# Attention masks added by TensorE as a matrix product instead of by VectorE, and the sink's exponential in one instruction

## The chip, the cores and the metric

The kernel runs on one core of one Trainium2 chip, as one program. The metric is the device time of one execution in microseconds (us). Before the change it was 1840.17 us, the median of 3 runs (1836.04 to 1841.17).

A core has engines with an instruction queue each, which run side by side and meet through semaphores: TensorE (PE: matrix products into the accumulation memory PSUM; PEld is its loading of the stationary operand), VectorE (DVE), ScalarE (ACT), GpSimd (POOL), and SyncE (SP), which here only starts transfers.

## The reference

Two transformer blocks of depth 2 over 256 tokens of width 1024, in fp32. The first block has a gated linear attention layer and a latent attention layer (MLA), the second two grouped-query attention layers (GQA). Every layer also attends to 256 memory tokens. Two kinds of attention are masked: MLA is causal, and the first GQA layer attends within a band of 128 positions and has a sink per head.

```python
# first block, layer 1 (MLA): 8 heads, key width 128 + 64 (rope), queries in blocks of 128
#   softmax over the keys with kpos <= qpos
# second block, layer 0: 12 heads of width 64, 3 key heads
def banded_attention(q, k, v, radius, sink=None):
    ...
    mask = abs(qpos - kpos) <= radius
    s = einsum(q, k) * ATTN_SCALE
    s = where(mask, s, -inf)
    m = maximum(max(s), sink)
    p = exp(s - m)
    denom = sum(p) + exp(sink - m)
    o = einsum(p, v) / denom
# second block, layer 1: the same heads, no mask and no sink
# memory attention: 4 heads in each layer, no mask and no sink
```

## The kernel before

The 256 tokens are two tiles (t = 0, 1) of 128 rows. All weights stream through in 534 units of 128 x 1024 numbers: SP loads a unit into `raw` (3 slots), ACT rounds it to `whi`, DVE forms the remainder `wlo` (6 slots each), and PE multiplies in three fp32r passes (`act_hi`*`whi`, `act_hi`*`wlo`, `act_lo`*`whi`). Work is written out by hand once per engine: each engine has a class `Stages` with a method per stage, and `model` calls them in the same order. The order on an engine is the order of that code, and the counts in the semaphore waits tie the engines together.

`attention(jobs)` is such a method on PE, ACT and DVE. A job is one head. There are four calls: 4 memory heads (gated linear layer), 4 memory heads and 8 causal heads (MLA), 4 memory heads and 12 banded heads (first GQA layer), and the same without mask (second GQA layer). The heads go through a pipeline of steps s = 0, 1, ...; the buffers `prob`, `top`, `inv`, `es` and the score banks `ps[:, j % 4]` hold 4 heads.

- **PE, step s** (lines 1886 to 1940): score products of head s, both query tiles (L1901; in MLA a second product for the 64 rope rows, L1904); transposes of the probabilities of head s-3 (L1925), which wait for `prob_ready`; product with the values of head s-4 (L1937), which waits for `probT_ready`. Where heads are 64 wide (both GQA layers), the scores of two heads are issued together at every even s, alternating between them: one head's operands lie in partitions 0 to 63, the other's in 64 to 127. A new score group waits until the exponentials of the head that used its bank are done. A plain fp32 product is two MATMUL instructions here.
- **DVE, step s** (lines 1450 to 1516): waits for the scores of head s (`score_done`). For a masked head it adds the mask to them and writes the sum into `prob` (L1465 causal, one instruction per tile; L1468 band, one instruction). Then the maximum (L1473, L1476), the negated and scaled maximum `top` (L1481, or L1488 and L1490 with a sink); after that the normalising of head s-2 (L1499 with a sink, L1501, L1504) and the low part of the output of head s-5 (L1513).
- **ACT, step s** (lines 905 to 953): waits for `top` of head s-1, then two exponentials (L924, each followed by a short instruction that reads its sum), with a sink one more small exponential before each of them (L921, into `es`); then the copy of the transposes of head s-4 from PSUM (L937, L941) and the high part of the output of head s-5 (L951).

For a masked head the exponential reads `prob` (SBUF), for another one the scores in PSUM. After the last heads PE goes on with the first output projection units (L1609), which are in the ring already.

Of the kernel before, what the change touches and what calls it, by code (L numbers as in the profile page):

```python
# [21 lines left out]
P = 128  # L22
# [242 lines left out]
def build(nc, units, x_in, mem_in, mem2_in, const_in, gain_in, row_in, alpha_in, post_in, out):  # L265
    NU = units.shape[0]
    with ExitStack() as ctx:
# [40 lines left out]
        alpha = sb("alpha", [GRANK, 512])  # L308
        lowT = sb("lowT", [GRANK, S])
# [72 lines left out]

        gla_pe = sem("gla_pe")
# [56 lines left out]
        def mla_jobs():  # L440
            jobs = []
            for h in range(MH):
# [4 lines left out]
                                 causal=True, mask=constant("causal"), sink=None, rms=("qn", h)))  # L447
            return jobs

        def gqa_jobs(b):  # L450
# [7 lines left out]
            for h in range(QH):  # L458
# [4 lines left out]
                                 mask=constant("band") if b == 0 else None,  # L463
# [148 lines left out]
        def _(act):  # L612
            class Stages:
# [197 lines left out]
                def gla(self):  # L811
                    act.wait_ge(params_landed, 48)
                    self.split(7)

# [94 lines left out]
                def attention(self, jobs, beside={}):  # L909
                    n, base = len(jobs), self.jobs  # L910
                    for s in range(n + 5):
                        if 1 <= s <= n:

                            j, job = s - 1, jobs[s - 1]
                            act.wait_ge(top_ready, base + j + 1)
                            for t in range(TT):
                                n_keys = keys_of(job, t)
                                src = (ps[:, j % NB, t * S:t * S + n_keys] if job["mask"] is None
                                       else prob[:, j % NB, t, 0:n_keys])
                                if job["sink"] is not None:  # L920
                                    nc.scalar.activation(es[:, j % NB, t:t + 1], job["sink"], ACT.Exp,  # L921
                                                         bias=top[:, j % NB, t:t + 1])
# [35 lines left out]
        def _(dve):  # L958
            V = nc.vector

            class Stages:
# [488 lines left out]
                def attention(self, jobs, beside={}):  # L1450
                    n, base = len(jobs), self.jobs
                    for s in range(n + 5):
                        if s < n:
# [4 lines left out]
                            if job["mask"] is not None:  # L1458
                                if j >= NB:
                                    dve.wait_ge(probT_done, base + j - NB + 1)  # L1460
                                mask = job["mask"].rearrange("p (t k) -> p t k", t=TT)
                                for t in range(TT):
                                    n_keys = keys_of(job, t)
                                    if job["causal"]:
                                        ins = V.tensor_tensor(prob[:, j % NB, t, 0:n_keys], src[:, t, 0:n_keys],  # L1465
                                                              mask[:, t, 0:n_keys], ALU.add)
                                if not job["causal"]:
                                    ins = V.tensor_tensor(prob[:, j % NB], src, mask, ALU.add)  # L1468
                                self.step(ins)
                                src = prob[:, j % NB]  # L1470
# [507 lines left out]
```

## Time and profile before

| | before |
|---|---|
| median of 3 runs | 1840.17 us (1836.04 to 1841.17) |
| profiled execution, first to last instruction (span) | 1837.2 us, mean granted clock 0.980 |
| PE busy | 1718.0 us (94%), 10778 matmul instructions |
| DVE busy | 1095.9 us (60%) |
| ACT busy | 899.6 us (49%) |
| POOL busy | 76.6 us (4%) |
| DMA | 289.20 MB, 157 GB/s over the span |
| chain that ended last, by engine | PE 81%, DVE 9%, ACT 5% |

In the rows of stretches below, each row has the stretch from start to end, its length, the busy time (and instructions) of PE, PEld, DVE, ACT and POOL, the granted share of TensorE's clock (PEclk: 1.00 is 2.4 GHz, 0.50 is 1.2 GHz), the busy share of the DMA engines and GB/s. In rows of a timeline stand the start, the time until the last of the x instructions ended, and in brackets how long the engine had stood idle and who ended it. The profile gives the profiled execution's span and no other time of it; the median stands 3.0 us above that span. The PE row counts a matmul as busy until its result is written, so a busy PE isn't one at its peak. The weights' products (L1609, L1675 to L1677, L1706) make up most of PE's time; the masked attention heads lie in two stretches, about 912 to 940 us (MLA) and 1244 to 1288 us (first GQA layer).

### The profile page before, as it was taken

How to read it: one execution, taken by the hardware profiler on the slowest of the kernel's cores; microseconds unless marked ns; L12 is line 12 of the kernel's file. 1: busy time of each engine (PE TensorE's matmuls, PEld its weight loads, DVE VectorE, ACT ScalarE, POOL GpSimd, SP SyncE). 2: the span in 40 equal slices, each digit the busy share in tenths (PEclk: the TensorE clock that was granted, in tenths of full speed). 3: DMA queues.
4: the chain of work that ended last, by engine and by line, in shares of the span. 5: the costliest groups of instructions: out<-in, count | busy, mean ns of one | idle time of the engine just before them, and what ended most of it. 6: DMA issues, size and time to landing. Idle time of an engine off the chain costs nothing.

```text
span 1837.2 us, 29340 instructions
## 1 busy us (share of the span) xinstructions
PE 1718.0 (94%) x10778; PEld 1516.3 (83%) x10778; DVE 1095.9 (60%) x1613; ACT 899.6 (49%) x1430; POOL 76.6 (4%) x99
## 2 busy tenths in 40 slices
PE   7999999889999999999799999996899998889998
PEld 6999887579999899987678999873699986579997
DVE  4555666455555655567765555558565556755554
ACT  5444453445444544445555444456544444754443
POOL 1000000000000100001201000000100000110000
PEclk9999999999999999999899999999999998999999
DMA  6655444245555455545224555550255553145553
GB/s 210 194 192 183 162 148 138 92 160 161 188 183 187 149 184 185 182 158 184 80 96 155 190 184 186 170 174 1 97 201 193 179 184 107 47 138 190 185 185 114
DMA packets 79654, 289.20 MB, mean 157 GB/s; under 512 B 8928, under 2 KB 9184, under 8 KB 79216
## 3 DMA queue, kind: packets, MB, share of 16 engines
q1 hardware_dynamic: 78272, 282.23, 46.4%
q0 software_dynamic: 1008, 5.24, 0.8%
q10 hardware_dynamic: 320, 1.01, 0.2%
q8 instruction: 34, 0.56, 0.1%
q14 instruction: 20, 0.16, 0.0%
HBM read 287.39 MB, written 1.05 MB: 157 GB/s over the span
## 4 chain that ended last, share of the span: by engine, by line
PE 81%; DVE 9%; ACT 5%; issue 2%; DMA 2%; POOL 1%; SPq 0%; DVEq 0%; ACTq 0%
PE ps L1706 18%; PE ps L1609 16%; PE ps L1677 13%; PE ps L1675 13%; PE ps L1676 13%; DVE wlo L981 2%; PE ps L1555 2%; PE ps L1937 2%; PE ps L1901 1%; DMA raw<-units 1%; ACT whi L637 1%; DVE inv L1476 1%; DVE act_lo L992 1%; ACT junk L660 1%; ACT act_hi L648 1%
## 5 line engine op out<-in xcount | busy, mean ns | idle before, releaser
L1675 PE MATMUL ps<-act_hi,whi 128*128 128x256 f32 x2112 | 603.1, 286 | 4.0 <-DVE wlo L981 3.1
L1676 PE MATMUL ps<-act_lo,whi 128*128 128x256 f32 x2112 | 599.8, 284 | 0.0
L1677 PE MATMUL ps<-act_hi,wlo 128*128 128x256 f32 x2112 | 599.7, 284 | 0.0
L1157 DVE TENSOR_TENSOR wlo<-raw,whi 128x1024 fp32r<-128x1024 f32 x358 | 437.0, 1221 | 177.9 <-ACT whi L777 177.7
L1675 PEld LDWEIGHTS ps<-act_hi,whi 128*128 128x128 f32 x2112 | 407.4, 193 | 10.9 <-DVE wlo L981 3.7
L777 ACT ACTIVATE whi<-raw 128x1024 fp32r<-128x1024 f32 x358 | 365.7, 1052 | 101.9 <-DMA raw<-units 100.9
L1676 PEld LDWEIGHTS ps<-act_lo,whi 128*128 128x128 f32 x2112 | 407.4, 193 | 4.7
L1677 PEld LDWEIGHTS ps<-act_hi,wlo 128*128 128x128 f32 x2112 | 407.2, 193 | 0.0
L981 DVE TENSOR_TENSOR wlo<-raw,whi 128x1024 fp32r<-128x1024 f32 x176 | 211.9, 1226 | 116.0 <-ACT whi L637 115.5
L1126 DVE TENSOR_TENSOR prob<-ps,prob 128x512 f32<-128x512 f32 x132 | 91.3, 692 | 252.8 <-PE ps L1677 252.6
L637 ACT ACTIVATE whi<-raw 128x1024 fp32r<-128x1024 f32 x176 | 180.9, 1055 | 119.2 <-DMA raw<-units 114.1
L756 ACT ACTIVATE sil<-prob 128x256 f32<-128x256 f32 x132 | 55.4, 420 | 343.5 <-DVE prob L1126 343.5
L1609 PE MATMUL ps<-whi,act_hi 128*128 128x512 f32 (+2 forms) x514 | 175.9, 403 | 18.4 <-DVE x L1206 6.3
L1609 PE MATMUL ps<-wlo,act_hi 128*128 128x512 f32 (+2 forms) x514 | 170.7, 393 | 0.0
L1609 PE MATMUL ps<-whi,act_lo 128*128 128x512 f32 (+2 forms) x514 | 170.1, 392 | 0.0
L1706 PE MATMUL ps<-whi,hid_hi 128*128 128x512 f32 x528 | 165.5, 395 | 2.1 <-DVE hid_lo L1132 2.1
L1706 PE MATMUL ps<-wlo,hid_hi 128*128 128x512 f32 x528 | 163.6, 391 | 0.0
L1706 PE MATMUL ps<-whi,hid_lo 128*128 128x512 f32 x528 | 163.1, 390 | 0.0
L1609 PEld LDWEIGHTS ps<-whi,act_hi 128*128 128x128 f32 x514 | 97.0, 194 | 44.9 <-issue 20.5
L759 ACT ACTIVATE hid_hi<-hid 128x256 fp32r<-128x256 f32 x132 | 55.1, 418 | 134.3 <-DVE hid L1120 134.3
L1706 PEld LDWEIGHTS ps<-wlo,hid_hi 128*128 128x128 f32 x528 | 99.1, 188 | 22.1
L1706 PEld LDWEIGHTS ps<-whi,hid_lo 128*128 128x128 f32 x528 | 99.1, 188 | 21.6
(187 smaller groups left out, 1522.2 us busy)
## 6 DMA issues: line engine op xcount, KB each, us to landing
raw<-units SPq DMA_DIRECT2D x534, 512.0 KB, 3.4
arena<-mem_in POOLq DMA_DIRECT2D x3, 1024.0 KB, 6.8
gpost<-post_in POOLq DMA_DIRECT2D x4, 512.0 KB, 4.8
x<-x_in SPq DMA_DIRECT2D x2, 512.0 KB, 4.6
out<-x SPq DMA_DIRECT2D x2, 512.0 KB, 3.2
const<-const_in ACTq DMA_DIRECT2D x1, 816.0 KB, 4.5
row<-row_in ACTq DMA_DIRECT2D x1, 134.0 KB, 5.1
const<-const_in SPq DMA_DIRECT2D x1, 64.0 KB, 3.0
```

The lines of the kernel that those rows point to most:

```text
L637: nc.scalar.activation(whi[:, u % RING, :], raw[:, u % RAW, :], ACT.Copy).then_inc(hi_ready, 1)
L756: nc.scalar.activation(sil[:, c % 2, :], gate_up_rms[:, c % 2, 0, :], ACT.Silu).then_inc(sil_ready, 1)
L759: nc.scalar.activation(hid_hi[:, c % 2, :], hid[:, c % 2, :], ACT.Copy).then_inc(hid_hi_ready, 1)
L777: nc.scalar.activation(whi[:, u % RING, :], raw[:, u % RAW, :], ACT.Copy).then_inc(hi_ready, 1)
L981: V.tensor_tensor(wlo[:, u % RING, :], raw[:, u % RAW, :], whi[:, u % RING, :].bitcast(F32), ALU.subtract).then_inc(lo_ready, 1)
L1126: V.tensor_tensor(gate_up_rms[:, c % 2], ps[:, 4 + c % 2, :].rearrange("p (e s) -> p e s", e=2), inv_rms.unsqueeze(1).to_broadcast([P, 2, ...
L1157: V.tensor_tensor(wlo[:, u % RING, :], raw[:, u % RAW, :], whi[:, u % RING, :].bitcast(F32), ALU.subtract).then_inc(lo_ready, 1)
L1609: ins = T.matmul(ps[:, bank, 0:b - a], a_part[:, t * P:(t + 1) * P], w_part[:, self.slot, w0 + a:w0 + b], start=k == 0 and s0, stop=k == n ...
L1675: T.matmul(out_, whi[:, slot, w], act_hi[:, k, :], start=k == 0, stop=False)
L1676: T.matmul(out_, whi[:, slot, w], act_lo[:, k, :], start=False, stop=False)
L1677: ins = T.matmul(out_, wlo[:, slot, w], act_hi[:, k, :], start=False, stop=k == KD - 1)
L1706: ins = T.matmul(ps[:, 2 * t + j, :], h_part[:, c % 2, tok], w_part[:, slot, j * 512:(j + 1) * 512], start=first and s0, stop=last and s1)
```

## The change

1. In the gated linear layer ACT makes four 128 x 128 fp32r arrays once, behind its first 7 weight units and ahead of an exponential over 1024 columns: the identity `eye`, the two pieces of the band mask that are not zero, and the triangular piece of the causal mask (both tiles use the same).
2. On PE each score group of a masked head gets one more product: `eye` (stationary) times the mask piece (moving, 128 columns), accumulated onto the 128 of the 256 score columns where the mask isn't zero. It's issued once per head and query tile, right behind that tile's score product: 2 for each of 8 heads in MLA, 2 for each of 12 heads in the first GQA layer. It spans all 128 partitions.
3. DVE doesn't add masks any more (L1465, L1468 go), and takes the maximum from PSUM. With the addition goes its wait on `probT_done`.
4. ACT takes the exponentials of masked heads from PSUM. The sink's exponential is one instruction over both tiles' columns instead of two.
5. PE waits once for the four arrays (`masks_ready`) ahead of a masked attention stage.

```diff
@@ -306,6 +306,9 @@
         gain = sb("gain", [P, GAIN_W])
         row = sb("row", [P, ROW_W])
         alpha = sb("alpha", [GRANK, 512])
+        eye = sb("eye", [P, P], F32R)
+        mask_band = sb("mask_band", [P, TT, P], F32R)
+        mask_causal = sb("mask_causal", [P, P], F32R)
         lowT = sb("lowT", [GRANK, S])
         decay = sb("decay", [P, 4 * GH])
         sums = sb("sums", [P, STAT_W])
@@ -380,6 +383,7 @@
         head_hi = sem("head_hi")
         head_lo = sem("head_lo")
 
+        masks_ready = sem("masks_ready")
         gla_pe = sem("gla_pe")
         gla_act = sem("gla_act")
 
@@ -444,7 +448,8 @@
                 jobs.append(dict(q=[m_k[:, t, h * P:(h + 1) * P] for t in range(TT)], k=m_kT[:, h, :],
                                  more=([m_qrT[r, h // 2, t * P:(t + 1) * P] for t in range(TT)], m_krT[r, :]),
                                  v=[m_v[:, t, h * MDV:(h + 1) * MDV] for t in range(TT)], rows=(0, MDV), kt=h,
-                                 causal=True, mask=constant("causal"), sink=None, rms=("qn", h)))
+                                 causal=True, mask=[(t * S + t * P, mask_causal[:]) for t in range(TT)],
+                                 sink=None, rms=("qn", h)))
             return jobs
 
         def gqa_jobs(b):
@@ -460,7 +465,8 @@
                 jobs.append(dict(q=[b_qT[r, h // 2, t * P:(t + 1) * P] for t in range(TT)], k=b_kT[r, g, :],
                                  more=None, v=[b_p[:, t, QKW + g * HD:QKW + (g + 1) * HD] for t in range(TT)],
                                  rows=(r.start, HD), kt=h // 2, causal=False,
-                                 mask=constant("band") if b == 0 else None,
+                                 mask=[(t * S + (1 - t) * P, mask_band[:, t, :]) for t in range(TT)]
+                                 if b == 0 else None,
                                  sink=row[:, ROW_AT["sink"] + h:ROW_AT["sink"] + h + 1] if b == 0 else None,
                                  rms=("bq", h) if b == 1 else None))
             return jobs
@@ -610,6 +616,13 @@
 
         @block.scalar
         def _(act):
+            def round_masks():
+                nc.scalar.activation(eye[:], ident, ACT.Copy)
+                band = constant("band")
+                for t in range(TT):
+                    nc.scalar.activation(mask_band[:, t, :], band[:, t * S + (1 - t) * P:t * S + (2 - t) * P], ACT.Copy)
+                nc.scalar.activation(mask_causal[:], constant("causal")[:, 0:P], ACT.Copy).then_inc(masks_ready, 1)
+
             class Stages:
                 u = used = 0
                 g = th = 0
@@ -811,6 +824,7 @@
                 def gla(self):
                     act.wait_ge(params_landed, 48)
                     self.split(7)
+                    round_masks()
 
                     act.wait_ge(gla_dve, 2)
                     self.step(nc.scalar.activation(at_arena(G_B, 1024), at_arena(G_B, 1024), ACT.Exp))
@@ -913,13 +927,11 @@
 
                             j, job = s - 1, jobs[s - 1]
                             act.wait_ge(top_ready, base + j + 1)
+                            if job["sink"] is not None:
+                                nc.scalar.activation(es[:, j % NB, :], top[:, j % NB, :], ACT.Exp, bias=job["sink"])
                             for t in range(TT):
                                 n_keys = keys_of(job, t)
-                                src = (ps[:, j % NB, t * S:t * S + n_keys] if job["mask"] is None
-                                       else prob[:, j % NB, t, 0:n_keys])
-                                if job["sink"] is not None:
-                                    nc.scalar.activation(es[:, j % NB, t:t + 1], job["sink"], ACT.Exp,
-                                                         bias=top[:, j % NB, t:t + 1])
+                                src = ps[:, j % NB, t * S:t * S + n_keys]
                                 scale = HD ** -0.5 if job["rms"] is None else query_scale(job)[:, t:t + 1]
                                 ins = nc.scalar.activation(prob[:, j % NB, t, 0:n_keys], src, ACT.Exp, scale=scale,
                                                            bias=top[:, j % NB, t:t + 1],
@@ -1455,19 +1467,6 @@
                             j, job = s, jobs[s]
                             dve.wait_ge(score_done, base + j + 1)
                             src = ps[:, j % NB, :].rearrange("p (t k) -> p t k", t=TT)
-                            if job["mask"] is not None:
-                                if j >= NB:
-                                    dve.wait_ge(probT_done, base + j - NB + 1)
-                                mask = job["mask"].rearrange("p (t k) -> p t k", t=TT)
-                                for t in range(TT):
-                                    n_keys = keys_of(job, t)
-                                    if job["causal"]:
-                                        ins = V.tensor_tensor(prob[:, j % NB, t, 0:n_keys], src[:, t, 0:n_keys],
-                                                              mask[:, t, 0:n_keys], ALU.add)
-                                if not job["causal"]:
-                                    ins = V.tensor_tensor(prob[:, j % NB], src, mask, ALU.add)
-                                self.step(ins)
-                                src = prob[:, j % NB]
                             if job["causal"]:
                                 for t in range(TT):
                                     ins = V.tensor_reduce(inv[:, j % NB, t:t + 1], src[:, t, 0:keys_of(job, t)],
@@ -1883,6 +1882,8 @@
 
                 def attention(self, jobs, beside={}):
                     n, base = len(jobs), self.jobs
+                    if any(job["mask"] is not None for job in jobs):
+                        pe.wait_ge(masks_ready, 1)
                     self.done = {job["kt"]: base + j + 1 for j, job in enumerate(jobs)}
                     self.banks_free()
                     self.all_taken()
@@ -1899,10 +1900,13 @@
                                     job, n_keys = jobs[j], keys_of(jobs[j], t)
                                     scores = ps[:, j % NB, t * S:t * S + n_keys]
                                     ins = T.matmul(scores, job["q"][t], job["k"][:, 0:n_keys], start=True,
-                                                   stop=job["more"] is None)
+                                                   stop=job["more"] is None and job["mask"] is None)
                                     if job["more"] is not None:
                                         ins = T.matmul(scores, job["more"][0][t], job["more"][1][:, 0:n_keys],
-                                                       start=False, stop=True)
+                                                       start=False, stop=job["mask"] is None)
+                                    if job["mask"] is not None:
+                                        at, mask = job["mask"][t]
+                                        ins = T.matmul(ps[:, j % NB, at:at + P], eye[:], mask, start=False, stop=True)
                                     if t == TT - 1:
                                         ins.then_inc(score_done, 1)
                         if s in beside:
```

PE in the first GQA layer, one pair of banded heads with what follows it, before (`arena` holds queries, keys and values; the first number of a shape is the rows of the result):

```order
L1901 MATMUL ps<-arena 128x256 x4
L1925 MATMUL ps<-const,prob 128x128 x4
L1937 MATMUL ps<-probT,arena 64x256 x2
L1925 MATMUL ps<-const,prob 128x128 x4
L1937 MATMUL ps<-probT,arena 64x256 x2
```

And the same place now:

```order
L1902 MATMUL ps<-arena 128x256
L1909 MATMUL ps<-mask_band,eye 128x128
L1902 MATMUL ps<-arena 128x256
L1909 MATMUL ps<-mask_band,eye 128x128
L1902 MATMUL ps<-arena 128x256
L1909 MATMUL ps<-mask_band,eye 128x128
L1902 MATMUL ps<-arena 128x256
L1909 MATMUL ps<-mask_band,eye 128x128
L1929 MATMUL ps<-const,prob 128x128 x4
L1941 MATMUL ps<-probT,arena 64x256 x2
L1929 MATMUL ps<-const,prob 128x128 x4
L1941 MATMUL ps<-probT,arena 64x256 x2
```

Four score products of two heads stood next to each other; now a mask product over all partitions stands behind each of them.

PE in MLA, one causal head, before:

```order
L1901 MATMUL ps<-arena 128x128
L1904 MATMUL ps<-arena 128x128
L1901 MATMUL ps<-arena 128x256
L1904 MATMUL ps<-arena 128x256
L1925 MATMUL ps<-const,prob 128x128 x3
```

And now:

```order
L1902 MATMUL ps<-arena 128x128
L1905 MATMUL ps<-arena 128x128
L1909 MATMUL ps<-mask_causal,eye 128x128
L1902 MATMUL ps<-arena 128x256
L1905 MATMUL ps<-arena 128x256
L1909 MATMUL ps<-mask_causal,eye 128x128
L1929 MATMUL ps<-const,prob 128x128 x3
```

The mask product comes in behind the 64-row rope product of each tile, ahead of the next product over all partitions.

## Rows read from the trace of the kernel before

**Rows 1.** Stretches of the first GQA layer: us, busy by engine, PEclk, DMA.

```profile
1244.35:1251.38 7.03, 5.43 (x25) 3.04 (x25) 5.06 (x16) 3.96 (x15) 0.00 (x0) 0.84 0.00 0
1251.38:1258.30 6.92, 5.09 (x26) 2.65 (x25) 5.85 (x19) 4.71 (x17) 0.00 (x0) 0.89 0.01 2
1258.30:1265.46 7.16, 5.33 (x25) 2.95 (x24) 5.35 (x16) 4.08 (x15) 0.00 (x0) 0.86 0.00 1
1265.46:1271.77 6.31, 4.47 (x25) 2.46 (x24) 5.90 (x19) 4.64 (x16) 0.00 (x0) 1.00 0.00 0
...
1278.08:1287.52 9.44, 6.19 (x33) 3.34 (x32) 8.60 (x30) 7.56 (x25) 0.00 (x0) 1.00 0.00 1
```

**Rows 2.** Busy time of a stretch: the eight causal heads' steps, MLA.

```profile
912.09:936.92 24.83, 24.83 (x122) 17.03 (x121) 17.56 (x69) 15.16 (x53) 0.00 (x0) 1.00 0.00 1
```

**Rows 3.** Timeline of DVE, first GQA layer: start, us, engine, line, operation.

```profile
1266.73 0.67 DVE L1468 TENSOR_TENSOR prob<-ps,const 128x512 f32<-128x512 f32 x1
1267.44 0.69 DVE L1476 TENSOR_REDUCE inv<-prob 128x2 f32<-128x512 f32 x1
...
1268.42 0.17 DVE L1490 TENSOR_SCALAR top<-inv 128x2 f32<-128x2 f32 x1
...
1269.99 0.69 DVE L1468 TENSOR_TENSOR prob<-ps,const 128x512 f32<-128x512 f32 x1
```

**Rows 4.** Timeline of ACT in the same cycle.

```profile
1268.63 0.29 ACT L921 ACTIVATE es<-row,top 128x1 f32<-128x1 f32 x1 [0.68 <-DVE top L1490]
...
1269.32 0.28 ACT L921 ACTIVATE es<-row,top 128x1 f32<-128x1 f32 x1
1269.51 0.49 ACT L924 ACTIVATE prob<-prob,top 128x256 f32<-128x256 f32 x1
...
1270.12 0.60 ACT L941 ACTIVATE probT<-ps 128x512 f32<-128x512 f32 x1
```

**Rows 5.** Timeline of PE in the same cycle (rows*columns of the array, then the operand).

```profile
1265.46 1.14 PE L1901 MATMUL ps<-arena 64*128 64x256 f32 x8
1266.54 0.66 PE L1925 MATMUL ps<-const,prob 128*128 128x128 f32 x4
...
1270.77 1.08 PE L1937 MATMUL ps<-probT,arena 128*64 128x256 f32 x4 [0.55 <-ACT probT L941]
1271.77 1.13 PE L1901 MATMUL ps<-arena 64*128 64x256 f32 x8
```

**Rows 6.** Timeline of PE in one causal head's step, MLA.

```profile
929.23 0.70 PE L1901 MATMUL ps<-arena 128*128 128x256 f32 x2
929.86 0.70 PE L1904 MATMUL ps<-arena 64*128 64x256 f32 x2
930.49 0.55 PE L1925 MATMUL ps<-const,prob 128*128 128x128 f32 x3
930.87 0.82 PE L1937 MATMUL ps<-probT,arena 128*128 128x256 f32 x4
931.53 0.28 PE L1901 MATMUL ps<-arena 128*128 128x128 f32 x1
```

**Rows 7.** Timeline of PE, fp32r products of 512 and 192 columns in turn.

```profile
834.28 0.50 PE L1609 MATMUL ps<-wlo,act_hi 128*128 128x512 f32 x2
834.62 0.50 PE L1609 MATMUL ps<-whi,act_lo 128*128 128x512 f32 x2
```

**Rows 8.** Timeline behind MLA's last causal scores, PE and DVE.

```profile
936.65 0.62 DVE L1465 TENSOR_TENSOR prob<-ps,const 128x128 f32<-128x128 f32 x2 [0.57 <-PE ps L1904]
...
937.30 0.61 DVE L1473 TENSOR_REDUCE inv<-prob 128x1 f32<-128x128 f32 x2
...
938.83 0.55 PE L1925 MATMUL ps<-const,prob 128*128 128x128 f32 x3 [1.08 <-DVE prob L1504]
```

**Rows 9.** Timeline of ACT where the change puts its four copies.

```profile
255.96 1.06 ACT L816 ACTIVATE arena<-arena 128x1024 f32<-128x1024 f32 x1 [2.33 <-DVE arena L1232]
```

**Rows 10.** Groups by line, operation and shape: ACT's 128x128 copies.

```profile
L937 ACT ACTIVATE probT<-ps 128x128 f32<-128x128 f32 x8 | 2.1, 266 | 0.0
```

## The prediction

> **What bounds the kernel now.** I read the shares by engine first: PE is busy for 94% of the span, DVE 60%, ACT 49%. So DVE work that goes is worth something only where PE waits for DVE, and PE work that comes costs wherever PE doesn't wait. That has to be read from the two masked stretches, not from the sums.
>
> MLA: over its causal heads PE is busy for the whole 24.83 us [rows 2], DVE for 17.56 of them. PE sets the pace there, a head's step takes 24.83 / 8 = 3.1 us, and DVE waits for PE, as its 0.57 us of idling before the addition shows [rows 8]. Only behind the last scores does PE wait for DVE (1.08 us at L1925 [rows 8]).
>
> First GQA layer: from one masked score group to the next it is 7.03, 6.92, 7.16, 6.31 and 6.31 us (the fifth reads like the fourth), then 9.44 us until the output projection starts [rows 1]. The first three have a PEclk of 0.84 to 0.89, so 2.2, 1.5 and 2.0 us of them ran at 1.2 GHz (twice the missing share times the length). At the full clock the pace is 6.31 us a pair, and it is DVE's: 5.90 us busy, two head steps of it in a row, the second starting 3.26 us behind the first (1266.73 to 1269.99 [rows 3]). PE is busy for 4.47 us of the 6.31 and waits.
>
> **MLA, part by part.** Removed: DVE's additions, about 0.65 us a head (936.65 to 937.30 [rows 8]). They lie beside PE, so for seven of eight heads they are worth 0.
> Added on PE: two mask products a head. First what a product costs when the occupied rows of the array change. Two MATMULs of 256 columns in the value product plus two of 128 take 0.66 us from start to start (930.87, 931.53 [rows 6]), that is 0.22 for 256 columns and 0.11 for 128. But the same pair of 256 columns takes 0.63 when it stands between a 128-row and a 64-row product (929.23, 929.86, 930.49 [rows 6]) instead of 0.44. So each change between 64 and 128 rows costs 0.2 us: about 0.09 until the array is empty and about 0.11 for a load of 128 columns that can't be hidden any more. The mask product comes behind the 64-row rope product, where a change to 128 rows stood anyway. The number of changes stays at four a head; what is added is the mask product's own slot. For a row of 128 columns whose load overlaps, the nearest rows are the transposes: three in 0.38 us with 0.06 of first load, 0.11 each [rows 6]. That is the load's time, and I take it: 2 x 0.11 = 0.22 a head.
> Bounds: the streaming alone. The fp32r passes over 512 and 192 columns follow each other in 0.34 us [rows 7], so 704 columns run near one per cycle of 2.4 GHz (0.29 us), and a narrow one isn't stretched; 128 columns are 0.05 us below. Above: as long as an fp32 MATMUL of 256 columns, 0.22 us.
> Seven heads: 7 x 0.22 = 1.5 us. At the last head the result comes later by the first mask (0.11) and by its own (0.11 of load and a drain that now ends later, 0.26 together), DVE is earlier by 0.65: PE's wait shrinks by 0.3. MLA: 1.5 - 0.3 = +1.2 us.
>
> **First GQA layer, part by part.** Removed from DVE: 0.71 us a head (1266.73 to 1267.44 [rows 3]). Removed from ACT: the second sink exponential, 0.19 us (1269.32 to 1269.51 [rows 4]), and 0.03 for reading PSUM instead of SBUF (an estimate; both kinds of exponential lie near 0.49).
> Added on PE: today the eight MATMULs of two heads take 1.08 us with the entry (1265.46 to 1266.54 [rows 5]), which is 8 x 0.11 + 0.2: the two heads run side by side in the halves of the array, since one alone needs 0.22 a piece. A mask product over 128 rows now stands behind each score product. So no two heads' products are neighbours, and every product stands behind a change of rows. Four score products at 0.63 = 2.5; four mask products at 0.09 + 0.11 + 0.05 = 0.26, less 0.15 for the last, behind which the 128-row transposes need no change: 0.9. The group takes 3.4 us instead of 1.08.
>
> The Trainium skill speaks to this (TensorEngine Tiling (Array Packing), section Tiling Modes): tiles of one mode run in parallel, a change of mode drains TensorE. It gives no price for the drain; the rows above do. The same skill (TensorE: Matmul & The Clock Gate, section on the back-to-back issue gap) gives an isolated gap of N/2.4 + 2.5 ns, 56 ns for 128 columns; by it the MLA term would be 0.8 us less. The transposes' 0.11 us speaks for the larger figure (loads in between), and I keep to the row.
>
> The new pace of a pair is the longest ring of waits: the group starts; the first head's scores are done after 3 x 0.63 + 2 x 0.26 and the last mask's 0.33 = 2.7 us; DVE 0.04 later takes maximum, sink and `top`, 1.15 us (1267.44 to the end of 1268.42's [rows 3]); ACT 0.04 later its exponentials, 1.49 (1268.63 to 1270.12) - 0.22 = 1.27 us, then the PSUM copy of an earlier head, 0.60 [rows 4]; PE 0.04 later that head's value product, 1.00 (1270.77 to 1271.77 [rows 5]), and the next group follows. Sum 6.85 us. DVE alone would need 6.31 - 2 x 0.72 = 4.9, PE alone 4.47 + 2.3 = 6.8 at most: the bound moves from DVE to PE with what PE waits for.
> First cycle: half of it ran at 1.2 GHz for 2.2 us because PE had idled before, which the change doesn't touch. What the new group does in those 2.2 us it would do in 1.1, so 3.4 becomes 4.5 instead of 2.0: the ring gives 6.85 + 1.1 = 8.0, against 7.03. The other four: 4 x 6.85 = 27.4 against 26.7 (6.92 + 7.16 + 6.31 + 6.31). I take the full clock for them, since PE will be busy for nearly the whole of each. Tail: its end hangs on the second head's DVE step. Its maximum will start 2.7 + 2.55 (the step without addition, 1267.44 to 1269.99) = 5.3 us after the group; today it starts at 4.53 + 0.72 = 5.25, behind an addition of its own. So 9.44 stays. Layer: +1.0 + 0.7 = +1.7 us.
>
> **The rest.** The four 128 x 128 copies on ACT: 4 x 0.27 [rows 10] = 1.1 us. ACT idles for 2.33 us before the exponential they precede [rows 9], and they lie in that wait (with the table load); cost 0, or 1.1 if that cover went. PE's wait for them is long met. The loss in each stretch passes on in full: what follows are projection units that are split already. Second GQA layer, memory heads and feed-forward layers: 0.
>
> **Sum.** 1837.2 + 1.2 + 1.7 = 1840.1 us for the span, 2.9 more; on the median of the runs 1840.2 + 2.9 = 1843.1 us, 0.16% slower. What a measurement of this kernel can tell from no change is about 0.3%, 5.5 us.
>
> **Rivals.**
> A. The heads lose their company but a change of rows costs nothing between a head's product and its mask (the mask's load slips in). The group is then 8 x 0.22 + 4 x 0.11 = 2.2, the first result after 1.85, the ring 6.0 us: one cycle of 7.2 and four of 6.0, against 33.7: -2.5; with MLA's +1.2 that is -1.3, 1838.9. The 0.63 of [rows 6], in both directions, speaks against it.
> B. Slower, by the clock. The group now holds half of a cycle; if the granted clock falls as it did in three cycles of five today [rows 1], it stretches by the full half of such a stretch, 1.7 us, instead of the 0.9 it costs a 1.08 us group. Two more stretches at 1.2 GHz: +3.4, 1846.5; three pass the 5.5 us. For it: PE's gaps between small products. Against it: PE waits less than before, and at 0.84 to 0.89 the clock fell after waits.
> C. Slower, by the mask product's own length: 0.22 instead of 0.05 of streaming. MLA 0.49 a head, +3.4 in all; the group 0.7 longer, its first result 0.5 later: ring 7.35, first cycle 8.6, four at 7.35, tail +0.5: +4.8. Sum +8.2, 1848.4. Speaks against it: [rows 7].
> D. Faster, as DVE's share would have it: masks cost PE nothing and heads stay side by side. First result after 1.1: ring 5.3, five cycles 27.5 instead of 33.7 (the first 6.3), tail -0.7, MLA -0.6: 7.5 less, 1832.7. The order of the code speaks against it: the mask product stands between the two heads.
>
> **How the numbers follow.** Forecast 0.66; A 0.09; B 0.13; C 0.08; D 0.04. Faster by over 0.3% is D and a little of A: 0.05. Slower by over 0.3%: C, some 0.08 of B, and 0.03 for the scatter of three runs (5 us between them before): 0.19. The rest, 0.76, is no change that can be told. The range from 1838.5 takes in most of A and reaches to 1848.5 over B and C; D stays out.
>
> **What the profile of the changed kernel would show.** The score line would stand as x2, mask x1, x2, mask x1 in the first GQA layer, 3.4 us from the group's start to the transposes, with PEld idling for "issue" before each; if it takes 2.2, A is right; if a mask stands for over 0.4 with its load, C. Pair cycles near 6.85 at PEclk 1.00; a PEclk under 0.95 in more than one of them is B. In MLA a step of 3.3 us instead of 3.1, still with PE busy throughout, and DVE idling 1.2 us or more a head. DVE's idling in the first GQA layer should grow from 0.4 to about 2.4 us a pair. ACT's four copies should stand in the wait at 252 us and leave its exponential where it was. I'm wrong in kind if the pair cycle falls under 6.3.

## The result and the profile after

The changed kernel took 1845.47 us as the median of 13 runs (1842.41 to 1854.46). The kernel before took 1838.94 beside it (13 runs, 1836.04 to 1841.17). The ratio is 1.0040, with a 95% interval of 1.0027 to 1.0052: 6.5 us more by the medians. I had forecast 1843.1 and "no change that can be told". The time lies in the forecast range. The rise is more than twice the 2.9 us forecast, and at 0.40% it's above the 0.3% that I had named as the least that can be told.

The page of the kernel after, shares by engine and the chain that ended last:

```profile
PE 1741.0 (94%) x10818; PEld 1530.7 (83%) x10818; DVE 1082.9 (59%) x1585; ACT 897.1 (49%) x1422; POOL 76.7 (4%) x99
...
PE 82%; DVE 8%; ACT 5%; issue 2%; DMA 2%; POOL 1%; SPq 0%; DVEq 0%; ACTq 0%
```

DVE was busy for 13 us less (1095.9 before), ACT for 2.5 less and PE for 23 more. The change does what it says, and the engine that got the work is the one the chain runs through. The 23 us are no price, though. This execution was one of the longer ones (1849.81 us, mean granted clock 0.973, against 1840.17 and 0.980 before), and it also ran at 1.2 GHz for longer in stages that the change doesn't touch. So I read the two masked stages by themselves.

**First GQA layer.** Stretches from one masked score group to the next and the tail (us, busy PE, PEld, DVE, ACT, POOL, PEclk, DMA share, GB/s), against [rows 1]:

```profile
1250.24:1261.35 11.11, 11.11 (x29) 5.81 (x28) 4.71 (x17) 5.26 (x18) 0.00 (x0) 0.54 0.01 2
1261.35:1268.18 6.83, 6.67 (x30) 3.64 (x29) 3.73 (x14) 2.76 (x10) 0.00 (x0) 1.00 0.00 0
1268.18:1275.00 6.82, 6.66 (x30) 3.63 (x29) 4.61 (x17) 4.13 (x15) 0.00 (x0) 1.00 0.01 1
...
1288.65:1297.91 9.26, 8.40 (x38) 4.52 (x37) 6.92 (x25) 6.48 (x21) 0.00 (x0) 1.00 0.00 0
```

Four cycles stand at 6.82 us and full clock, PE busy in all but 0.16 of each: the pace is PE's now, where it was DVE's at 6.31. The first cycle took 11.11 us at a PEclk of 0.54 (twice the missing 0.46 times 11.11 is 10.2 us at 1.2 GHz; the trace's own record of the clock has 10.24). That one row is what the forecast did not have.

A full-clock group (PE, the layer's third cycle: start, us, engine, line, operation, and in brackets what it waited for), against [rows 5]:

```profile
1268.18 0.70 PE L1902 MATMUL ps<-arena 64*128 64x256 f32 x2
1268.80 0.33 PE L1909 MATMUL ps<-mask_band,eye 128*128 128x128 f32 x1
1269.06 0.70 PE L1902 MATMUL ps<-arena 64*128 64x256 f32 x2
...
1271.61 0.62 PE L1929 MATMUL ps<-const,prob 128*128 128x128 f32 x4
1272.17 1.08 PE L1941 MATMUL ps<-probT,arena 128*64 128x256 f32 x4
...
1273.99 1.08 PE L1941 MATMUL ps<-probT,arena 128*64 128x256 f32 x4 [0.16 <-ACT probT L953]
1275.00 0.48 PE L1902 MATMUL ps<-arena 64*128 64x256 f32 x1
```

From start to start a score product takes 0.62 and its mask product 0.26; the group takes 3.43 us (1268.18 to 1271.61), where 3.4 was forecast. DVE and ACT in the same cycle, against [rows 3, 4]:

```profile
1270.93 0.69 DVE L1475 TENSOR_REDUCE inv<-ps 128x2 f32<-128x512 f32 x1 [1.87 <-PE ps L1909]
...
1273.49 0.69 DVE L1475 TENSOR_REDUCE inv<-ps 128x2 f32<-128x512 f32 x1
```

```profile
1272.12 0.29 ACT L931 ACTIVATE es<-top,row 128x2 f32<-128x2 f32 x1 [2.17 <-DVE top L1489]
...
1273.34 0.59 ACT L953 ACTIVATE probT<-ps 128x512 f32<-128x512 f32 x1
```

DVE waits 1.87 us for the group, then its maximum is late by 2.75 from the group's start (2.7 forecast), the second by 5.31 (5.3). ACT takes 1.22 from its exponential to the copy out of PSUM (1.27). Then PE waits 0.16 for that copy, so the ring closes as drawn.

The tail took 9.26 us where 9.44 stood. The last head's exponentials and the copy out of PSUM behind them (ACT), before and after:

```profile
1284.52 0.29 ACT L921 ACTIVATE es<-row,top 128x1 f32<-128x1 f32 x1 [0.94 <-DVE top L1490]
...
1285.89 0.57 ACT L941 ACTIVATE probT<-ps 128x512 f32<-128x512 f32 x1
```

```profile
1295.15 0.30 ACT L931 ACTIVATE es<-top,row 128x2 f32<-128x2 f32 x1 [0.49 <-DVE top L1489]
...
1296.25 0.59 ACT L953 ACTIVATE probT<-ps 128x512 f32<-128x512 f32 x1
```

Counted from the group's start, they begin at 6.50 us instead of 6.44, but the copy follows after 1.10 us instead of 1.37. PE's last value product before the output projection waits for that copy and starts at 8.25 instead of 8.44.

The same group in the first cycle:

```profile
1249.65 0.66 PE L1929 MATMUL ps<-const,prob 128*128 128x128 f32 x4 [2.40 <-DVE prob L1503]
1250.24 1.22 PE L1902 MATMUL ps<-arena 64*128 64x256 f32 x2
1251.39 0.47 PE L1909 MATMUL ps<-mask_band,eye 128*128 128x128 f32 x1
...
1256.32 1.07 PE L1929 MATMUL ps<-const,prob 128*128 128x128 f32 x4
1257.33 1.97 PE L1941 MATMUL ps<-probT,vm 128*64 128x256 f32 x4
```

PE had waited 2.40 us for DVE, the granted clock fell as the group began, and it stayed at 1.2 GHz for 10.24 us: every product of the group takes near twice its time (6.08 us in all), and so do most of the transposes and value products behind it.

**MLA.** Seven of the eight causal heads' steps as a stretch, then PE at two mask products, then the tail, against [rows 2, 6, 8]:

```profile
917.23:941.27 24.04, 24.04 (x124) 17.14 (x123) 11.91 (x50) 12.70 (x44) 0.00 (x0) 1.00 0.00 1
```

```profile
930.08 0.33 PE L1909 MATMUL ps<-mask_causal,eye 128*128 128x128 f32 x1
930.25 0.52 PE L1929 MATMUL ps<-const,prob 128*128 128x128 f32 x3
...
933.56 0.33 PE L1909 MATMUL ps<-mask_causal,eye 128*128 128x128 f32 x1
```

```profile
940.46 0.62 DVE L1472 TENSOR_REDUCE inv<-ps 128x1 f32<-128x128 f32 x2 [1.46 <-PE ps L1909]
...
945.27 0.55 PE L1929 MATMUL ps<-const,prob 128*128 128x128 f32 x3 [0.57 <-DVE prob L1503]
```

The seven steps take 24.04 us, and 22.35 in before's trace read the same way: 0.24 more for each (3.59, 3.48 and 3.27 where 3.35, 3.24 and 3.03 stood). PE is busy throughout, DVE idles 1.46 us before its maximum, and PE's wait behind the last scores fell from 1.08 to 0.57. From the last scores to the output projection it is 5.58 instead of 5.92: +1.7 - 0.3 = +1.3 us.

**ACT's copies**, in the wait of [rows 9]:

```profile
253.16 0.29 ACT L620 ACTIVATE eye<-const 128x128 fp32r<-128x128 f32 x1
253.36 0.49 ACT L623 ACTIVATE mask_band<-const 128x128 fp32r<-128x128 f32 x2
253.75 0.29 ACT L624 ACTIVATE mask_causal<-const 128x128 fp32r<-128x128 f32 x1
...
256.86 1.06 ACT L830 ACTIVATE arena<-arena 128x1024 f32<-128x1024 f32 x1 [1.51 <-DVE arena L1244]
```

They end with 1.51 us of waiting left: hidden.

### The profile page after: what moved, and what is told of

Same layout as the page of the kernel before. It is cut to its first block, busy times and chain, and to the rows that moved or that the text cites. A ratio compares the mean times of both kernels' runs of the same rounds, so it can differ in the third digit from the quotient of the medians.

```text
span 1847.9 us, 29364 instructions
## 1 busy us (share of the span) xinstructions
PE 1741.0 (94%) x10818; PEld 1530.7 (83%) x10818; DVE 1082.9 (59%) x1585; ACT 897.1 (49%) x1422; POOL 76.7 (4%) x99
## 3 DMA queue, kind: packets, MB, share of 16 engines
q1 hardware_dynamic: 78272, 282.23, 46.7%
HBM read 287.39 MB, written 1.05 MB: 156 GB/s over the span
## 4 chain that ended last, share of the span: by engine, by line
PE 82%; DVE 8%; ACT 5%; issue 2%; DMA 2%; POOL 1%; SPq 0%; DVEq 0%; ACTq 0%
PE ps L1705 18%; PE ps L1608 16%; PE ps L1676 13%; PE ps L1674 13%; PE ps L1675 13%; DVE wlo L993 2%; PE ps L1941 2%; PE ps L1902 2%; PE ps L1554 2%; DMA raw<-units 1%; ACT whi L650 1%; DVE act_lo L1004 1%; ACT junk L673 1%; ACT act_hi L661 1%; ACT prob L936 1%
```

## The experiments

My theory after the result: the sums of slots and drains were right, and the surplus is one stretch at 1.2 GHz which the first band-masked group makes longer. Its rivals are a constant cost elsewhere (the copies, the sink, MLA), or chance. In all that follows, ratios are to the kernel before on the same chip, with 95% intervals. "DVE masks" means the additions as before, with the sink still in one instruction.

**Each part alone, and the change again.**

```diff
 # e1: the first GQA layer's band back on DVE
-mask=[(t * S + (1 - t) * P, mask_band[:, t, :]) for t in range(TT)]
+mask=None, add=constant("band") if b == 0 else None
 # e2: MLA's causal mask back on DVE
-mask=[(t * S + t * P, mask_causal[:]) for t in range(TT)]
+mask=None, add=constant("causal")
 # e3: both; only the sink's edit and the copies stay
```

> Masks by TensorE for the causal heads alone; the band is added by VectorE as before, the sink's exponential is one instruction. Steps theory (the two added mask products and the changes of rows cost what their slots take, the rest is the granted clock in the first GQA layer): MLA's heads take 3.3 us a step, +1.2 us against the kernel before, first GQA layer as before. Rival (the changed program is slower in many places, by a lower clock anywhere): +3 us or more here too.

> Masks by TensorE for the banded heads alone; the causal mask is added by VectorE as before. Steps theory: pair cycle 6.8 us, +1.7 us against the kernel before if the clock in the first cycle is as before. Clock theory: the first masked score group starts at 1.2 GHz and, with its gaps, keeps the core there for about 10 us instead of 3.4; then the first cycle takes 11 us instead of 7 and the kernel is 4 to 5 us slower than before.

> All masks added by VectorE as before; what is left of the change is the four copies on ScalarE, TensorE's one wait for them and the sink's single exponential. If the copies lie in ScalarE's wait and VectorE sets the pace of the first GQA layer: no change, within 0.5 us, pair cycle 6.3. If the copies or the shifted phase of the clock cost something: +1 us or more.

> The changed kernel once more, unchanged, for a second profile and more runs beside the same runs of the kernel before. Steps theory: pair cycles of 6.82 us again. Clock theory: the first masked pair cycle of the first GQA layer again holds about 10 us at 1.2 GHz and takes 11 us. If that was chance, it takes about 8 us this time.

Measured, against 1838.98 (32 runs): e1 1839.42 (0.9997, 0.9985 to 1.0009); e2 1843.83 (1.0023, 1.0013 to 1.0033); e3 1838.11 (0.9995, 0.9984 to 1.0006); e4 1846.0 (1.0043, 1.0027 to 1.0059). So the copies and the sink cost nothing that can be told, and neither does MLA's part, whose +1.3 us is below what a median shows. The band masks carry the rise. Their first cycles, in e1, e3, e2 and e4:

```profile
1245.29:1252.00 6.71, 5.97 (x25) 3.32 (x24) 5.29 (x17) 3.85 (x14) 0.00 (x0) 0.75 0.01 2
```

```profile
1245.99:1252.83 6.84, 5.51 (x25) 3.12 (x25) 4.87 (x15) 3.59 (x14) 0.00 (x0) 0.82 0.00 0
```

```profile
1246.47:1257.05 10.58, 10.58 (x29) 5.44 (x28) 4.28 (x15) 4.53 (x18) 0.00 (x0) 0.58 0.00 0
```

```profile
1245.50:1256.64 11.14, 11.14 (x30) 5.78 (x29) 4.71 (x17) 5.25 (x18) 0.00 (x0) 0.54 0.01 2
```

All four stand behind the same wait of 2.4 us. In e1 and e3, with DVE masks, the layer had 3.41 us at 1.2 GHz. In the three profiles with the changed kernel's group (e2, e4 and the one above) it had 10.24 in one piece, and no profile with DVE masks on the first heads has more than 3.41 in one. Chance alone is unlikely. The whole layer, memory heads to output projection, took 46.1 and 46.7 us in e1 and e3, 52.6 and 52.7 in e2 and e4: about +6. The medians of the two pairs that differ by the band masks alone say the same: e2 less e3 is 5.7 us, e4 less e1 is 6.6. So the long stretch can't be rare in the executions that were only timed.

The profile of before, on which I had forecast, has 48.6 us for this layer with 6.83 at 1.2 GHz. Its second and third cycle were longer than those of e3 (6.92 and 7.16 against 6.04 and 6.30), and I had set the new ones against them.

**How long the group is.** Three kernels change what stands in the masked group. e6 puts both heads' scores of a tile ahead of both masks, e7 issues each mask product twice (masked scores come out doubly negative), and e8 gives a head one mask product of 256 columns for both tiles, behind all of its scores, in a bank that only the first tile's product opens.

```diff
 # e6: per tile, scores of both heads, then masks of both
+for j in range(s, s + pair):
+    job = jobs[j]
     if job["mask"] is not None:
 # e7: twice
+T.matmul(ps[:, j % NB, at:at + P], eye[:], mask, start=False, stop=False)
 # e8: the bank is opened once; one mask product a head
+ins = T.matmul(scores, job["q"][t], job["k"][:, 0:n_keys], start=t == 0 or not masked, ...)
...
+out_, mask = bank[:, P:3 * P], mask_band[:].rearrange("p t k -> p (t k)")
+T.matmul(out_, eye[:], mask, start=False, stop=True).then_inc(score_done, 1)
```

> The changed kernel with another order within a masked group of the first GQA layer: per tile both heads' scores, then both masks. Drain theory (each change between 64 and 128 rows costs 0.2 us, neighbours of different heads run side by side): group 1.95 us instead of 3.43, first result 0.75 us earlier, pair cycle 6.1 instead of 6.82; 3 us faster than the changed kernel at the same clock, more if the clock recovers earlier in the first cycle. Rival (the mask products themselves are what costs, whatever stands next to them): group 3 us or more.

> The changed kernel with every mask product issued twice in a row (the masked scores become twice as negative, nothing else changes). It prices the product's own slot without a further change of rows. Slot theory: 0.11 us each, bound by the load of eye: MLA step 3.27 to 3.49 us, pair cycle 6.82 to 7.15, about 3 us slower than the changed kernel. Streaming theory (0.05 us each): 3.38 and 7.0. If each product paid the whole 0.26 us: 3.79 and 7.6, 7 us slower.

> Masks by TensorE with few changes of rows: in a masked group both tiles' scores of the head or the pair first (in MLA all products over 128 rows, then all over 64), then one mask product of 256 columns per head for both tiles. Drain theory: group of the first GQA layer about 1.4 us, ring and pair cycle 5.6; MLA loses two of its four changes of rows, step 2.75 us; 5 to 7 us faster than the kernel before. Rival (VectorE or another engine then bounds the pair cycle at 6.0 or more, or the cycle is long by the clock): no faster than before by more than 3 us.

Measured, against 1838.93 (17 runs): e6 1839.46 (1.0008, 0.9995 to 1.0020); e7 1850.68 (1.0068, 1.0055 to 1.0081); e8 1830.93 (0.9956, 0.9943 to 0.9969). PE in a full-clock group of e7, then of e8:

```profile
1281.78 0.33 PE L1909 MATMUL ps<-mask_band,eye 128*128 128x128 f32 x1
1281.94 0.28 PE L1910 MATMUL ps<-mask_band,eye 128*128 128x128 f32 x1
1282.15 0.70 PE L1902 MATMUL ps<-arena 64*128 64x256 f32 x2
```

```profile
1262.40 1.13 PE L1903 MATMUL ps<-arena 64*128 64x256 f32 x8
1263.47 0.51 PE L1923 MATMUL ps<-mask_band,eye 128*128 128x256 f32 x2
1263.81 0.60 PE L1941 MATMUL ps<-const,prob 128*128 128x128 f32 x4
```

In e7 the time from one score product to the next is 0.99 us, 0.11 more than the 0.88 with one mask; in MLA its steps are 0.22 longer for two more products (3.49 against 3.27). A mask product's slot is 0.11. e7 as a whole lies 11.7 us above before, 5.2 more than the changed kernel, where the slots alone would have made 3. In e8 the heads run side by side again, the group takes 1.41 us instead of 3.43, the cycle 5.56 instead of 6.82; e6 lies between (6.06, 6.1 expected). MLA's step in e8 is 2.81: 0.22 below before, though it has mask products and before had none, since there are two changes between 64 and 128 rows a head instead of four. e8 as a whole came out 8.0 us faster than before, where I expected 5 to 7.

The Trainium skill says that changing the tiling mode drains TensorE (TensorEngine Tiling (Array Packing), Key Properties) and gives no price; the runs agree that a change costs time, 0.2 us between 64 and 128 rows (0.16 in e12 below). How that splits into drain and unhidden load is an estimate; the trace shows only the sum. The Trainium skill also says that a product that opens an accumulation clears the written-bits of the whole bank and leaves later ones to overwrite where the bit is clear (PSUM — Partial Sum Buffer, The four PSUM rules); e8 is built on that: its second tile's products land in columns of a bank that the first tile's product has opened. No trace shows the bits.

The length of the stretch at 1.2 GHz that begins at about the first group goes with the group. First cycles of e6, e7 and e8:

```profile
1245.35:1253.49 8.14, 8.14 (x30) 4.54 (x29) 4.61 (x17) 4.92 (x18) 0.00 (x0) 0.58 0.01 3
```

```profile
1245.45:1258.24 12.79, 12.79 (x34) 6.88 (x33) 4.33 (x15) 5.04 (x18) 0.00 (x0) 0.50 0.00 1
```

```profile
1244.89:1251.29 6.40, 6.18 (x28) 3.71 (x27) 4.58 (x17) 4.26 (x16) 0.00 (x0) 0.73 0.02 4
```

It lasted 3.41 us in before, e1, e3 and e8 (products of one kind next to each other), 6.83 in e6, 10.24 in the three with the changed kernel's group and 13.65 in e7, where two more stretches of 3.41 followed later in the layer (the second cycle took 8.61 us). From e8 over e6 and the changed kernel to e7 two things grow together: the length of the group, and the part of it that goes to changes of rows and unhidden loads. Which of them holds the clock down isn't shown, and e6, e7 and e8 have one profile each.

**Taking the half clock away.** In e5, twenty fp32r products of 256 columns into a free bank stand ahead of the transposes that PE waits for just before the first masked group. In e9, DVE masks the first two banded heads, and TensorE the other ten and MLA.

```diff
 # e5
+if s == 3 and any(job["sink"] is not None for job in jobs):
+    for _ in range(20):
+        T.matmul(ps[:, 6, 0:S], eye[:], mask_band[:].rearrange("p t k -> p (t k)"), start=True, stop=True)
 # e9
-if b == 0 else None,
+if b == 0 and h >= 2 else None,
+add=constant("band") if b == 0 and h < 2 else None,
```

> The changed kernel, and in the first GQA layer twenty products of 256 columns (eye times the band mask, into a free bank, read by nobody) on TensorE in the 2.4 us wait ahead of the first transposes, just before the first masked group. Clock theory (TensorE had stood still, so the masked group starts at 1.2 GHz and its gaps keep it there): the core stays at 2.4 GHz, the first masked cycle takes about 7 us instead of 11, the kernel is about 4 us faster than the changed one, near 1841.5. Rival (the masked groups' gaps alone bring the clock down, or the cycle is long for another reason): first cycle 8 us or more, half-clock time in the stage as before, no gain or 1 us of loss.

> The changed kernel, but VectorE adds the band mask for the first two banded heads; the other ten and the causal heads stay on TensorE. It takes the gapped group out of the place that runs at 1.2 GHz. Clock theory (a gapped group that starts at 1.2 GHz prolongs that state to 10 us): first masked cycle near 6.8 us, half-clock time in the stage 3.4 to 6.8 us, the kernel 3 to 4 us faster than the changed one. Rival (the first gapped group in line, wherever it starts, brings a long slow stretch): the stretch moves to the next cycle, which then takes 10 us.

Measured: e5 1845.11 (5 runs; 1.0034, 1.0021 to 1.0047), e9 1842.95 (1.0019, 1.0010 to 1.0028; before 1839.44). The first cycle of e5, then the first two of e9:

```profile
1254.51:1262.68 8.17, 8.17 (x29) 4.44 (x28) 4.70 (x17) 4.96 (x18) 0.00 (x0) 0.79 0.00 1
```

```profile
1253.91:1260.73 6.82, 5.98 (x25) 3.33 (x24) 5.30 (x17) 3.85 (x14) 0.00 (x0) 0.75 0.01 4
1260.73:1268.90 8.17, 8.17 (x29) 4.44 (x28) 5.31 (x19) 5.37 (x19) 0.00 (x0) 0.79 0.00 0
```

With PE kept busy, e5's group ran at full clock (3.44 us). The clock still fell 3.5 us after the group's start, though for 3.41 us only. e9 had two such stretches: one in its first cycle, as with DVE masks, and one that began 3.5 us after the start of its first group with TensorE's masks, which itself ran at full clock. So the wait before the group isn't the whole cause: in both profiles a fall came behind the first such group although it had met the full clock. Where it met 1.2 GHz, the stretch was the long one. The later groups of the same shape brought none (cycles of 6.82 us in both), and I can't say why.

The layer is 49.7 us instead of 52.7, in both kernels. In e9 that shows in the median too: it lies 3.5 us above before's, the changed kernel's 6.5. In e5 it doesn't: I expected about 1841.5 and got 1845.11, 6.2 above before, in five runs with one at 1850.8. The gain in the layer is shown in one profile of each, and e5's total doesn't confirm it.

**Fewer changes of rows without TensorE's masks, and the filling alone.** e10 is e8 with the filling in both GQA layers. e12 has DVE masks and only reorders MLA's products, both 128-row ones of a head ahead of both 64-row ones (its lines are shortened here). e13 has DVE masks and the filling.

```diff
 # e12
+for t in range(TT):   # behind both first products
+    ins = T.matmul(ps[:, s % NB, t * S:t * S + n_keys], job["more"][0][t], job["more"][1][:, 0:n_keys],
+                   start=False, stop=t == TT - 1)
 # e10, e13 (e13 also waits for masks_ready, since the filling reads the masks)
+if s == 3 and jobs[0]["rows"][1] == HD:   # then the twenty products of e5
```

> The kernel with one mask product per head, and the twenty filling products ahead of the first transposes in both GQA layers. If the fill keeps the core at 2.4 GHz there: first token cycle of the second GQA layer 4.9 instead of 5.8 us, first masked cycle of the first one 5.6 instead of 6.4, the kernel 1 to 2 us faster than without the fill. If the slow stretch only falls later, as it did in the changed kernel with the fill: no gain.

> All masks by VectorE (as before, with the single sink exponential); in MLA a head's score products are issued over 128 rows for both tiles and then over 64 rows for both, which takes two of the four changes of rows away and adds nothing. Drain theory: MLA step 3.03 - 0.4 = 2.63 us, 2.5 us faster than before at the same clock. Rival (the 0.2 us is not the change of rows but belongs to a product's start in a new output region): 3.03 stays.

> All masks by VectorE (as before, with the single sink exponential), and the twenty filling products ahead of the first transposes in both GQA layers. If the fill holds the clock up as it did beside the single masks: second GQA layer's first token cycle 4.9 instead of 5.8, first masked cycle 6.1 instead of 6.8, half-clock time in both stages 0, 1.5 to 2 us faster than before. If it helps only where TensorE is then busy: the slow stretch falls into a later cycle, no gain.

Measured: e10 1828.74 (0.9945, 0.9932 to 0.9958), the fastest, 10.7 us below before's 1839.44; e12 1834.02 (0.9974, 0.9962 to 0.9986); e13 1835.42 (0.9979, 0.9970 to 0.9987), both against 1839.94. A cycle of e10, and an MLA step of e12:

```profile
1242.71:1248.14 5.43, 4.68 (x27) 2.74 (x26) 4.58 (x17) 4.25 (x16) 0.00 (x0) 1.00 0.02 5
```

```profile
925.11:927.81 2.70, 2.70 (x16) 1.95 (x15) 2.14 (x10) 1.87 (x7) 0.00 (x0) 1.00 0.00 0
```

MLA's step is 2.70 us instead of 3.03 where 2.63 was expected: two changes of rows fewer, 0.16 each. One later step took 2.92, with PE waiting. The rival, by which 3.03 would stay, is out. The kernel is 5.9 us faster (2.6 to 7.0 by the interval), more than the 2.5 expected. In its profile MLA's seven steps and tail are 2.6 us shorter than before's; another 1.4 against e3 is the first GQA layer, which had no half clock in this execution. The rest I haven't located.

e10 and e13 had no half clock in the attention of either GQA layer. In the second one, all the profiles without filling but that of e7 had 3.41 us of it, and a first cycle of 5.8 us for token heads where e10 and e13 have 4.84, as expected: 1.0 us. In the first one e12, without filling, had none either. So of e13's 4.5 us (2.4 to 5.5 by the interval, 1.5 to 2 expected) I can't say how much is the filling's: the stretches come and go between executions.

## Why the prediction was near and yet short

- **The total.** The time fell in a range that I had drawn up to 1848.5 to take in B and C, and that is luck in part. With more runs before's median also came out 1.2 us lower than the one I started from. The rise of 6.5 us is B's 6.3, which I gave 0.13, and not the forecast's 2.9. By my mark of 0.3% the kernel is slower by what can be told, which I gave 0.19.
- **What bounds the kernel** held: MLA is PE's, the layer was DVE's and became PE's. DVE's 13 us were worth nothing by themselves.
- **MLA, +1.2:** right, +1.3. Steps +0.24 for +0.22, the tail -0.34 for -0.3. The slot of 0.11 that I chose over the streaming alone is what e7 measured, 0.11 and 0.22 for two.
- **A change of rows, 0.2 us, and the group of 3.4:** right (3.43). e6, e8 and e12 take changes away and get the time back, e12 at 0.16 for each. Rival A (they cost nothing, ring 6.0) is out, and so are C (0.22 of streaming: score to score would have been 1.05 us, not 0.88) and D (heads side by side).
- **The ring, 6.85:** right, 6.82. The tail was to stay and was 0.18 shorter: I hung it on DVE alone and left out what ACT saves behind DVE's `top`, forecast as 0.22 in the ring and measured as 0.27 there.
- **Copies and sink, 0:** right. At full clock e3's cycle is 6.31 us, as before, and the likely reason is that the sink's 0.19 lies on ACT, beside DVE's pace.
- **The failed step: the first cycle.** "Half of it ran at 1.2 GHz for 2.2 us because PE had idled before, which the change doesn't touch." I priced it at 8.0 us; it took 11.1. The wait before it is untouched, but the slow stretch isn't a fixed piece of time: it lasted 3.41 us with paired products and 10.24 with the changed group. At full clock this cycle would take 6.82, so the half clock costs 4.3 us there, where I had given 1.1. That is rival B's mechanism, but where B had two stretches more in later cycles, it was one, much longer, in the first; my mark for B ("under 0.95 in more than one of them") didn't fire.
- **A second error, of the baseline.** The four other cycles went from 26.7 to 27.3 against the one profile I had. Against the cycles of e3 (24.96) they are 2.3 more. In before, cycles two and three held a second stretch of 3.41 us that e1, e3, e12 and e13 don't have. It was most likely chance of that execution, and I booked it as lasting.

Together, e4 against e3: first cycle +4.3 (6.84 to 11.14), four cycles +2.3, tail -0.2, the memory heads ahead -0.5 (5.44 to 4.98; both values occur with either kind of masks). They make +6.0; with MLA's +1.3 it is 7.3 us, against 6.5 (5.0 to 9.6 by the interval). What stays open is why the changed group holds the clock down for longer, and whether it does so in every execution. Three profiles of three agree, and the other runs were only timed.

## What to carry to other kernels

Moving work from a waiting engine to TensorE is cheap by its columns and dear by its neighbours: count the changes of occupied rows that it makes and the pairs it separates, at up to 0.2 us a change, before counting columns. Put products over the same rows next to each other, and one wide mask product behind them instead of a narrow one behind each; the same idea that cost 6.5 us here then gained 8, part of it in MLA, where the new order also beats the kernel before. When a forecast rests on one profile, take the stretches at half clock out of the baseline first, then ask separately what the new shape does to them.

## What the runs showed of the hardware beyond that

- TensorE can count as busy for the whole of a stretch (11.11 us of 11.11) and be granted 1.2 GHz for 10.24 of it. The Trainium skill describes a kernel whose short idling between groups of MATMULs makes the clock fall again and again (TensorE: Matmul & The Clock Gate, A second HAM failure mode); here the clock didn't fall again and again, and the rows of the stretch show no idling at all. The stretch was shorter with fewer changes of rows (6.83 us in e6, 3.41 in e8) and longer with doubled mask products (13.65 in e7).
- With TensorE's wait filled by 20 products (2.5 us), the group behind it ran at 2.4 GHz in all three kernels that did so (e5, e10, e13); without filling only e12's did. The filling cost nothing: PE waited there for DVE anyway, and from the memory heads to the group it stayed at 4.99 us in e13, 4.98 in e1.
- The runs of the changed kernel lie by their mean granted clock: 1842.4 us at 0.981, 1844 to 1847 at 0.975 to 0.977, 1851.6 at 0.973, 1854.5 at 0.971. They spread over 12 us. The kernel before spread over 5 us in the 13 runs beside them, but over 12 in the 32 runs beside e1 to e4.
